# Latent attention with one wait per staging buffer, and an early output projection that begins two steps sooner and ends four later

## The reference

```
# first stack, differential attention: 8 heads, two softmaxes each
p = softmax(q1 k1^T) - lambda * softmax(q2 k2^T);  o = rms_norm(p @ v) * subln
x = x + concat(o) @ w_o
# second stack, latent attention: 8 heads, 64 + 32 columns of q and k
q = (rms_norm(q_lat) @ w_uq);  k, v = (rms_norm(kv_lat) @ w_ukv);  rope on 32 columns
o = softmax(mask(q k^T * 96**-0.5)) @ v
```

## Time and profile before

| | |
|---|---|
| median of 3 runs | 3766.67 us (3766.53 to 3769.91) |
| profiled execution | 3767.52 us, its span 3765.7 us |
| PE busy over the span | 3578.3 us, 95% |
| DVE, ACT, POOL busy | 44%, 29%, 31% |
| differential attention | 0 to about 623 us |
| starts of the two latent attentions' softmax loops | 2803.75 and 3483.33 us |

### The profile page before, as it was taken

The page is one execution under the profiler, slowest core; times in us unless marked ns, Lnnn a source line. Parts: engine busy times, 40 slices in busy tenths (PEclk is TensorE's granted clock), DMA queues, the critical chain, the costliest instruction groups (busy, mean ns, idle before and its releaser), DMA issues. The chain is left out here.

```text
span 3765.7 us, 44248 instructions
## 1 busy us (share of the span) xinstructions
PE 3578.3 (95%) x17776; PEld 2823.7 (75%) x17776; DVE 1639.2 (44%) x1917; ACT 1085.3 (29%) x1647; POOL 1179.7 (31%) x688
## 2 busy tenths in 40 slices
PE   7999999999999999999999999899989979998997
PEld 6777777888888888788888888787645768764566
DVE  4666655412121259642111113565646441374653
ACT  2455533201010116521010111215436311343540
POOL 2454541333333346432332332222202122230211
PEclk9999999999999999999999999999989989999998
DMA  4244331111111121211111111131042121213311
GB/s 161 93 140 138 116 132 61 56 49 46 50 47 48 67 73 56 84 45 50 50 45 50 50 45 45 51 128 59 32 129 57 62 101 40 76 34 87 96 62 62
DMA packets 81854, 270.36 MB, mean 72 GB/s; under 512 B 9616, under 2 KB 11568, under 8 KB 81712
## 3 DMA queue, kind: packets, MB, share of 16 engines
q1 hardware_dynamic: 56912, 197.07, 15.9%
q10 hardware_dynamic: 17888, 46.16, 3.6%
q0 software_dynamic: 6912, 25.17, 2.0%
HBM read 216.19 MB, written 47.97 MB: 70 GB/s over the span
## 5 line engine op out<-in xcount | busy, mean ns | idle before, releaser
L696 POOL CAST held_hi<-held_raw 128x1024 fp32r<-128x1024 f32 (+1 forms) x158 | 172.5, 1092 | 1076.3 <-PE tk_acc L195 560.5
L195 PE MATMUL tk_acc<-tk_a_hi,held_hi 128*128 128x512 f32 x1280 | 396.2, 391 | 4.4 <-POOL held_lo L698 4.4
L195 PE MATMUL tk_acc<-tk_a_hi,held_lo 128*128 128x512 f32 x1280 | 394.8, 390 | 0.0
L195 PE MATMUL tk_acc<-tk_a_lo,held_hi 128*128 128x512 f32 x1280 | 394.7, 390 | 0.0
L698 POOL TENSOR_TENSOR held_lo<-held_raw,held_hi 128x1024 fp32r<-128x1024 f32 (+1 forms) x158 | 378.1, 2393 | 12.7
L858 ACT ACTIVATE tk_sq<-tk_r 128x1024 f32<-128x1024 f32 x64 | 67.9, 1060 | 1067.1 <-DVE tk_r L993 1067.1
L195 PE MATMUL tk_acc<-tk_b_hi,held_hi 128*128 128x512 f32 x1200 | 369.5, 389 | 0.0
L195 PE MATMUL tk_acc<-tk_b_hi,held_lo 128*128 128x512 f32 x1200 | 369.4, 389 | 0.0
L195 PE MATMUL tk_acc<-tk_b_lo,held_hi 128*128 128x512 f32 x1200 | 369.4, 389 | 0.0
L962 DVE TENSOR_TENSOR xT<-tk_acc,xT 128x1024 f32<-128x1024 f32 x80 | 98.0, 1225 | 566.6 <-PE tk_acc L195 566.2
L195 PEld LDWEIGHTS tk_acc<-tk_a_hi,held_hi 128*128 128x128 f32 x1280 | 240.7, 188 | 56.4 <-POOL held_lo L698 5.2
(11 more groups left out here) (412 smaller groups left out, 6967.8 us busy)
## 6 DMA issues: line engine op xcount, KB each, us to landing
held_raw<-in_w_trunk SPq DMA_DIRECT2D x154, 512.0 KB, 3.2
da_w_mod<-in_ada_w POOLq DMA_DIRECT2D x48, 512.0 KB, 3.7
pj_w_raw<-in_w_in SPq DMA_DIRECT2D x44, 512.0 KB, 3.3
held_raw<-in_w_qkv SPq DMA_DIRECT2D x24, 512.0 KB, 3.8
x_dram<-xT ACTq DMA_DIRECT2D x24, 512.0 KB, 4.6
ma_w_raw<-in_w_out SPq DMA_DIRECT2D x16, 512.0 KB, 4.0
xT<-x_dram SPq DMA_DIRECT2D x16, 512.0 KB, 6.5
xT<-in_xT SPq DMA_DIRECT2D x13, 512.0 KB, 8.9
```

The lines of the kernel that those rows point to most:

```text
L195: last = pe.matmul(self.acc[:, u, s * HALF:(s + 1) * HALF], w[:, u, k, :], h[:, k, s * HALF:(s + 1) * HALF], start=(k == order[0] and part ...
L696: pool.tensor_copy(pn.hi[:, u, at:, :], pn.raw[:, u, at:, :]).then_inc(sems[f"w_hi{u}"], 1)
```

## The change

In the differential attention the fill of the output projection begins at step 49 in place of 51 and ends with step 67 in place of 63. ACT makes the high parts of the five heads (`head_high`, behind the exponentials of step 49), POOL only the low parts, and does so between its two weight splits. Each reload has a semaphore of its own. The three parts of an item stand by part and no more by chunk, the low part of the heads last, and the first two items are interleaved so that their low parts come behind both items' other parts (`wo_unit`). Sums and their order aside, nothing else in the arithmetic changes.

In the latent attention the staging places change: the first pair's q and k go to the even half of pr, the second's to pts, the third's to the odd half. Each pair of stores has its own semaphore, and ACT waits for one just before it first writes the buffer. SP stores the second pair behind the first pair's loads, and the loads of the first output weights go behind those of the second pair.

```diff
             made = [4, 5, 0, 6, 1, 7, 2, 8, 3, 9]
-            home = [ab[:, 0, 0, :], ab[:, 0, 1, :], pts[:, 0, :], pts[:, 1, :], pr[:, 1, 0, :], pr[:, 1, 1, :],
-                    pr[:, 0, 0, :], pr[:, 0, 1, :], more[:, 0, :], more[:, 1, :]]
-            group = [None, None, 0, 0, 1, 1, 2, 2, 2, 2]
+            home = [ab[:, 0, 0, :], ab[:, 0, 1, :], pr[:, 0, 0, :], pr[:, 0, 1, :], pts[:, 0, :], pts[:, 1, :],
+                    pr[:, 1, 0, :], pr[:, 1, 1, :], more[:, 0, :], more[:, 1, :]]
...
-                    for at in range(4, 6):
-                        keep(at)
-
                     for u in range(units):
...
                         if u == 1:
-                            for at in range(6, 10):
+                            for at in range(4, 10):
                                 keep(at)
                             sync.wait_ge(sems["lat_sum"], n_lat)
-                            load(0)
                             sync.wait_ge(sems["lat_st1"], 64)
...
                     def exps(t, m):
...
+                        if t < 2 and m == 0:
+                            act.wait_ge(sems["lat_st2" if t else "lat_st0"], 64)
...
                     def copies(t, m):
...
+                        if t == 0 and m == 0:
+                            act.wait_ge(sems["lat_st1"], 64)
...
-                    for j, n in enumerate((64, 64, 128)):
-                        act.wait_ge(sems[f"lat_st{j}"], n)
...
-        AHEAD, FROM = W_O_AHEAD, 51
+        AHEAD, FROM = W_O_AHEAD, 49
...
-            steps = nb - FROM
+            steps = nb + 4 - FROM
             return n_out * EACH * min(max(t - FROM, 0), steps) // steps
+        def wo_unit(unit):
+
+            if unit < 4 * AHEAD:
+                return divmod(unit, 2 * AHEAD)
+            if unit < 6 * AHEAD:
+                return (unit - 4 * AHEAD) // AHEAD, 2 * AHEAD + unit % AHEAD
+            return divmod(unit, EACH)
+
+        def wo_done(i):
+            return 5 * AHEAD if i == 0 else EACH * (i + 1)
...
                         if hp == pairs and j == 0:
-                            for u in range(2):
-                                split(pairs, 0, u)
+                            split(pairs, 0, 0)
                             for u in range(AHEAD):
-                                head_split(u)
+                                head_low(u)
+                            split(pairs, 0, 1)
...
+                    def head_high(u):
+
+                        act.wait_ge(sems[f"o_ld{u}"], 16)
+                        act.activation(oh_hi[:, u, :], oT[:, u, :], ACT.Copy).then_inc(sems["oh_hi"], 1)
...
                         scale_weights(t)
+                        if t == FROM - 1:
+                            for u in range(AHEAD):
+                                head_high(u)
```

More of the change, by code:

```diff
@@ L1750, in mixed_back @@
             "z_in0", "z_in1", "gated", "o_hi", "o_lo", "s_hi", "s_lo", "x_sq", "acc", "w_uv", "lat_sum", "lat_out", "lat_st0",
-            "lat_st1", "lat_st2", "tab", "kpe", "rot", "rot_st"] + [f"x_ld{n}" for n in range(DK)]
+            "lat_st1", "lat_st2", "lat_st3", "tab", "kpe", "rot", "rot_st"] + [f"x_ld{n}" for n in range(DK)]
         with stage(nc, tag, names) as (sems, sb, ps):
@@ L1861, in _ @@
                         sync.dma_start(zg[:, u % 2, :], self.proj[P_GATES + u]).then_inc(sems[f"z_in{u % 2}"], 16)
+                        if u == 1:
+                            load(0)
                         if u:
@@ L2150, in attention_layer @@
             "silu", "mod_scaled", "mod_added", "mod_used", "mod_landed0", "mod_landed1",
-            "oh_hi", "oh_lo", "wo_sum", "wo_x", "wo_added", "wo_st"]
+            "oh_hi", "oh_lo", "wo_sum", "wo_x", "wo_added", "wo_st"] + [
+            f"o_ld{u}" for u in range(W_O_AHEAD)]
         def groups(t):
@@ L2183, in wo_third @@
             return wo_cut(t) + (wo_cut(t + 1) - wo_cut(t)) * n // 3
+        def wo_unit(unit):
[6 more added lines that the diff above has]
+            return 5 * AHEAD if i == 0 else EACH * (i + 1)
         def wo_due(t):
-            return [i for i in range(n_out) if wo_third(t - 1, 1) < EACH * (i + 1) <= wo_third(t, 1)]
+            return [i for i in range(n_out) if wo_third(t - 1, 1) < wo_done(i) <= wo_third(t, 1)]
         with nc.sbuf_tensor("oh_hi", [P, DK, S], F32R) as oh_hi, nc.sbuf_tensor("oT", [P, DK, S], F32) as oT:
@@ L2307, in reload @@
                             sync.wait_ge(sems[f"o_st{f}"], 16 * (u + 1))
-                        sync.dma_start(oT[:, u, :], self.o_dram[u]).then_inc(sems["o_ld"], 16)
+                        sync.dma_start(oT[:, u, :], self.o_dram[u])\
+                            .then_inc(sems[f"o_ld{u}" if u < AHEAD else "o_ld"], 16)
                     def residual(n):
@@ L2332, in _ @@
                     sync.wait_ge(sems["wo_st"], 16 * (DK - 5))
-                    sync.wait_ge(sems["o_ld"], 16 * (units - 2))
+                    sync.wait_ge(sems["o_ld"], 16 * (units - 2 - AHEAD))
                 @block.gpsimd
@@ L2384, in out_split, with head_low @@
                             .then_inc(sems[f"w_split{u}"], 1)
-                    def head_split(u):
-                        pool.wait_ge(sems["o_ld"], 16 * AHEAD)
-                        pool.tensor_copy(oh_hi[:, u, :], oT[:, u, :]).then_inc(sems["oh_hi"], 1)
+                    def head_low(u):
                         pool.wait_ge(sems["oh_hi"], u + 1)
@@ L2464, in fill_out @@
                         for unit in range(a, b):
-                            i, at = divmod(unit, EACH)
+                            i, at = wo_unit(unit)
                             p, h = divmod(i, 2)
-                            kk, part = divmod(at, 3)
+                            part, kk = divmod(at, AHEAD)
                             if at == 0:
@@ L2474, in fill_out @@
                             if i == 0 and part == 0:
+                                pe.wait_ge(sems["oh_hi"], kk + 1)
+                            elif i == 0 and part == 2:
                                 pe.wait_ge(sems["oh_lo"], kk + 1)
-                            wt, x = ((w_hi, oh_hi), (w_hi, oh_lo), (w_lo, oh_hi))[part]
+                            wt, x = ((w_hi, oh_hi), (w_lo, oh_hi), (w_hi, oh_lo))[part]
                             last = pe.matmul(X[:, h, :], wt[:, p % 2, kk, :], x[:, kk, h * HALF:(h + 1) * HALF],
@@ L2697, in _ @@
                                                   ALU.subtract))
-                    for t in range(-1, nb + 4):
+                    for t in range(-1, nb + 5):
                         natural(t - 1)
```

7 lines of the change are left out of this document (3 added, 4 removed).

## The result

The changed kernel takes 3743.1 us (median of 4 runs, 3735.41 to 3746.55), the kernel before 3767.2 us beside it (4 runs, 3766.53 to 3769.91): a ratio of 0.9934, 95% interval 0.9921 to 0.9946, which is 24 us less.

A forecast was written before the change was run, and what follows sets the result against it. PE, busy 95%, was taken as the bound, losing time to waits and lower clock at three places. Stage -16 and latent attention -11 (both layers) sum to -27 us: 3767.5 to 3740.5, 3740 beside the median; range 3730 to 3756.

The forecast's parts named there:

- Head: Differential attention, steps 49 to 51: PE waits of 1, 1, 1 and 0.3 us, step 51 ending at 517.5.
- Steps 52 to 63: Differential attention: softmax chain stays hidden behind the thinner fill, 1 us of waits, ending at 592 us.
- Rival 4: Differential attention, steps 52 to 67: softmax chain shows through the thin fill, kernel slower at 3800 us; chance 0.03.
- Tail: End of the first stage: 51 units cover the 4.58 us norm wait; trunk starts about 609, not 623.35: -14.5 us.
- The unused matmuls' 1.5 us: Trunk's start: PE keeps its clock without the 4.58 us wait, so unused matmuls take 1.5 us less (bounds 0 and 2.9).
- The loads' issue: Latent attention: loads wait for the rope stores to land, taken as 2789.5 us, instead of issuing from 2791.73 on.
- rival 1: Latent attention: loads no earlier, only table load and store wait gained, -5 both layers, sum -21, 3746 us; chance 0.15.
- The loads' landing: Latent attention: about 1.2 of the 12.0 us from issue to landing go away; landing about 2800.3, 3.4 us earlier.
- The table load ahead of the maximum: Latent attention: table load comes ahead of the wait for DVE; with the late store wait gone, -2.5 us.
- The clock of the first scores: Latent attention's first scores: 3.5 us instead of 6.9 at full clock; half of that 3.4 us charged.
- Rivals 2, 3 and 5: 3: rivals 1 and 2 both, or moved stores late, 3756 to 3763, 0.08; 5: whole kernel, no tellable change, 0.05.
- rival 2: Differential attention's head split collides, PE at low clock till 514: stage -8, sum -19, 3748 us; chance 0.17.

The follow-up runs named there:

- the run with the stores first: Changed kernel, but SP stores the second pair ahead of the first pair's loads, as before; 3753.93 us, ratio to the kernel before 0.9957.
- the kernel with GpSimd's heads: Changed kernel, but POOL instead of ACT makes the heads' high parts, each ahead of its low part; 3753.55 us, 0.9961 of the kernel before.
- The changed kernel's second run: Changed kernel unaltered, timed again with the last experiments; 3743.37 us against 3767.86 for the kernel before, ratio 0.9935.

## Why the prediction was right, and where not

The forecast was 3740 us for 3743; the sum of -27 us stands against -28.0 in the edited stretches and -24 in the medians. The nearness of -28.0 is partly luck: the first stage gave 2.4 us less than said, and the latent stretches of this one run 3.4 us more. Step by step:

**Head.** Said: waits of 1 (fourth unit), 1 (`combine` of step 50), 1 (unit 24) and 0.3 (unit 30), end of step 51 at 517.5. Found: 0.45 for the high part and 0.52 for `combine` at the fourth unit, 1.58 at step 50, none at the 24th and 30th, end at 518.5. Both engines were in time: with the 1.9 us taken off, the transposes of step 49 began at 500.9 (said 500.5) and the second panel was split at 514.2 (said 513.6). The waits come to 2.55 us for the 3.3 said, and their place was not as said: I charged one us for two held instructions of step 50; `combine` cost 1.58 there and 0.52 in step 49. The us that the head is late is therefore not a wait. Steps 49 to 51 run from 499.14 to 520.14, 21.0 us with 18.45 busy; the forecast, 20.3 us with 3.3 of waits, left 17.0 for PE's own matmuls, which was 1.4 too little. The 21.1 busy us from 490 to 515, for the over 23 said, have 3.9 us of waits beside them, 1.4 of them for ACT's copies in step 48, as before. With these 1.4 and its own 3.3 the forecast left no room for 23. DVE and POOL, and DVE once more without POOL beside it:

```profile
499.77 3.02 DVE L2655 SCALAR_TENSOR_TENSOR da_pr<-da_pr,da_st 128x768 f32<-128x768 f32 x1
...
507.68 2.74 DVE L2655 SCALAR_TENSOR_TENSOR da_pr<-da_pr,da_st 128x512 f32<-128x512 f32 x1
...
513.83 2.53 DVE L2655 SCALAR_TENSOR_TENSOR da_pr<-da_pr,da_st 128x256 f32<-128x256 f32 x1
...
554.27 1.02 DVE L2655 SCALAR_TENSOR_TENSOR da_pr<-da_pr,da_st 128x768 f32<-128x768 f32 x1
```

```profile
499.27 13.39 POOL L2400 TENSOR_TENSOR oh_lo<-oT,oh_hi 128x1024 fp32r<-128x1024 f32 x5
```

The same 768 columns take 3.02 us beside the subtractions and 1.02 without, and 256 columns still 2.53; the subtractions take 13.39 / 5 = 2.68 us each instead of 2.35. A duration that hardly depends on the columns points to a wait for the other engine's instruction. The rule of the Trainium skill, SBUF — State Buffer, section "SBUF: two separate sides", that these two lock a shared port pair for a whole instruction, agrees with these rows. The subtractions are slowed as well.

**Steps 52 to 63.** Said: the chain stays hidden, last values done at 592. Found: 591.4 + 1.7 = 593.1, the one us of the head again; the only wait for `combine` is 0.4 us, though one of 0.9, for an `add_out`, is over the 0.5 that I gave as the limit. Rival 4 (the chain shows through) is refuted, with 6.2 us a step as forecast.

**Tail.** The norm's wait is hidden as said, the output transposes come at 604.6 for 603.6 and the unused matmuls at 609.8 for 609. The last store of x sets the barrier, 0.6 us behind ACT's end, for the 0.5 said. Measured alone the tail is 5.2 us, for the 7 that I gave as that end of the range.

**The unused matmuls' 1.5 us: wrong.** I thought PE would keep its clock without the 4.58 us wait. They take 9.28 us as before (9.27): the granted clock was 0.86 from 608 to 611.7, with the 3.12 us barrier wait in it, and 0.69 over the matmuls. The bound of 0 was the right end. With this and the us of the head, the stage is -13.6 for -16.

**The loads' issue: wrong.** I took 2789.5, 2.2 us sooner, from the bytes moved. From the rope stores' issue to the loads' it is 9.57 us before (2782.16 to 2791.73), 9.45 after (2765.97 to 2775.42), and between 9.4 and 9.6 in all the other kernels that keep this order: this is how long those stores take to land, and the queue did wait for it in the kernel before too. In this step rival 1 was right.

**The loads' landing: too small.** I took 1.2 us off the 12.0; found are 2.7 (12.0 to 9.3), 3.1 by the run with the stores first. I had only counted the bytes in flight as the loads were issued, at half.

**The table load ahead of the maximum: wrong.** It stands behind ACT's wait for DVE in every kernel here, until an instruction without a wait is put ahead of it. Of the 2.5 us counted for this and the stores, the stores' share came, 1.1 us (the load follows the maximum's end by 0.08 us instead of 1.21), and the table load's 1.3 us did not.

**The clock of the first scores: too small.** I charged half of 3.4 us. In this window the granted clock is 0.53 before, near the lower level (1.2 GHz), and 1.00 after, the higher (2.4 GHz); the first fence is of before, the second of after:

```profile
2803.75:2810.70 6.95, 6.92 (x8) 2.47 (x8) 1.22 (x1) 0.73 (x1) 0.00 (x0) 0.53 1.04 392
```

```profile
2784.70:2788.40 3.70, 3.66 (x8) 1.39 (x8) 1.23 (x2) 0.41 (x1) 2.00 (x1) 1.00 1.02 412
```

So the latent part, -11 by the ratio, is right in size and made partly of other terms. In layer 1, 6.6 us up to the table load: 3.7 less waiting of PE (5.23 to 1.55; said 3.4), 1.8 of clock up to the maximum's end (5.01 to 3.22 us behind the scores' start; said 0.85, half of the 1.7 charged), and 1.1 of the stores' wait (said 2.5 with the table load). Said were 6.8 up to the first exponential, of which 5.5 were carried to the stage. That these misses nearly cancel is luck. Part of the 3.7 us is this run's: in the others with the same code the wait is 1.9 to 3.4 us, as the rope stores are issued 8.7 to 10.6 us ahead of the x14 value products, and 10.6 in the run shown. That is part of why the latent stretches differ by up to 6 us among kernels with the same latent code. Another part is the clock, which the last section shows.

Rivals 2, 3 and 5 are refuted by the windows and the ratio; the head came through at full clock. What rival 2 described, an early start that collides, is what the kernel with GpSimd's heads did.

What stays open: how much of the 2.7 to 3.1 us in landing is the stores' bytes and how much their place in the queue, why the rope chain's start moves against the value products from run to run, and what besides the wait decides the clock of the first scores.

## What to carry to other kernels

On a queue whose loads release the bound engine, put every store that nobody waits for soon behind them: moving four stores of 256 KB gave 3 us in the loads' landing, and up to as much again in the clock of the matmuls behind the shorter wait. What a wait costs is its distance from the next thing that would hold the engine (here 1.2 us behind the maximum, of a wait of 10.83 us), and two runs are compared from that same point, not from one further back that moves between runs. Work that fills an engine's gaps has to be ready at the first gap, so give its preparation to the engine that is free then, and judge a gain of 3 us by the stage's length over several kernels, not by one.

## What the runs showed of the chip

- The clock after a wait of PE, first layer: the eight matmuls took 3.67 us, full clock, after waits of 1.55 to 2.94 us in eight runs; 5.37 after 3.44 and 3.46 us; 6.2 to 6.9 after 5.2 to 6.5 us. The second layer shows that the wait alone does not decide it: 3.67 us after 1.10 to 2.06 us in four runs, but 5.37 already after 2.17 to 3.13 us in six, and 6.0 to 6.8 after 5.3 to 6.1 us. From 2.2 to 2.9 us both were seen. The changed kernel's second run has both, 2.94 us with full clock in the first layer and this in the second:

```profile
3459.50 5.37 PE L1934 MATMUL ma_sc<-xT 104*128 104x512 f32 x8 [2.17 <-DMA xT<-mkpe_dram]
```

- In that run's first layer the clock was 1.00 over the eight and 0.50 from 2792.5 to 2799, behind one more wait of 2.18 us. The windows:

```profile
2786.70:2790.40 3.70, 3.67 (x8) 1.44 (x8) 1.23 (x1) 0.37 (x1) 0.66 (x1) 1.00 1.03 420
2792.50:2799.00 6.50, 6.42 (x16) 4.19 (x17) 2.70 (x5) 2.81 (x5) 0.00 (x0) 0.50 1.05 299
```

- The loads that wait for the pair of 512 KB stores of 8 x 16 x 1024 were issued 9.4 to 9.6 us behind the stores' issue in eleven kernels, whether other stores stood between or not; where large loads were issued at once behind them, what waited for the pair came after 10.8 us.
- The changed kernel's first latent stretch was 167.6 us in one run and 170.4 in another. In that stretch several of the experiments above differ from it by no more.
